# Transformer mixer layers on one core: order of one gather, one weight load and one weight split

## What is computed

```python
def _token_mix(h, w_in, w_out, gm_ln_g, gm_w_s, gm_b_s, da_lambda, da_sub_g, cmp_pe, cmp_w1, cmp_w2, lam_init):
    z = h @ w_in
    ...
    y_a = _gmlp_sgu(gu, gv, gm_ln_g, gm_w_s, gm_b_s)
    ...
    y_b = _diff_attention(dq, dk, dv, lam, da_sub_g, lam_init)
    y_c = _nsa(nq, nkc, nvc, nks, nvs, nkw, nvw, ng, cmp_pe, cmp_w1, cmp_w2)
    return jnp.concatenate([y_a, y_b, y_c], axis=-1) @ w_out

def _compress(x, pe, w1, w2):          # inside _nsa, for keys and for values
    ...
    blocks = x[:, :, idx] + pe
    flat = blocks.reshape(blocks.shape[0], blocks.shape[1], nc, CMP_LEN * HEAD_DIM_2)
    return jax.nn.silu(flat @ w1) @ w2
```

## Time and profile before

| | us |
|---|---|
| median of 3 runs | 2785.9 (2785.36 to 2786.52) |
| the profiled execution | 2786.57 |
| its span in the trace | 2785.2 |
| TensorE busy in it | 2715.7 |
| VectorE busy | 1667.7 |
| ScalarE busy | 1024.0 |

### The profile page before, as it was taken

How to read it: one execution, slowest core, us unless ns; L and a number is a source line. 1 busy time by engine, 2 the same in 40 slices (tenths; PEclk the granted TensorE clock), 3 DMA queues, 4 the chain that set the end, 5 groups by cost and what they waited for, 6 DMA issues and landing times.

```text
span 2785.2 us, 35300 instructions
## 1 busy us (share of the span) xinstructions
PE 2715.7 (98%) x14529; PEld 2222.0 (80%) x14529; DVE 1667.7 (60%) x3377; ACT 1024.0 (37%) x1745; POOL 15.8 (1%) x47
## 2 busy tenths in 40 slices
PE   8999999999999999899999999999999889999999
PEld 5788888898888897666888889888888666888888
DVE  6776565357767356777776746753355677633334
ACT  4642232444222244454422224322243455432223
POOL 1000000000000000000000000000000000000000
PEclk9999999999999999999999999999999999999999
DMA  7246333224555232201455524532232210123231
GB/s 248 91 167 183 106 98 96 72 91 167 200 190 170 93 107 84 94 18 46 166 182 186 192 83 147 193 130 97 93 115 84 88 46 31 61 92 106 91 102 65
DMA packets 340360, 325.24 MB, mean 117 GB/s; under 512 B 9442, under 2 KB 332774, under 8 KB 340200
## 3 DMA queue, kind: packets, MB, share of 16 engines
q1 hardware_dynamic: 340116, 322.97, 35.5%
q10 hardware_dynamic: 84, 0.02, 0.0%
HBM read 320.87 MB, written 2.10 MB: 116 GB/s over the span
## 4 chain that ended last, share of the span: by engine, by line
PE 89%; DVE 7%; ACT 2%; SPq 1%; issue 0%; DMA 0%; DVEq 0%
PE bank L529 25%; PE bank L531 24%; PE bank L530 24%; PE bank L571 3%; PE bank L557 2%; PE bank L559 2%; PE bank L558 2%; PE bank L2313 1%; PE bank L2342 1%; DVE w_lo L497 1%; PE bank L1367 1%; PE bank L1357 1%; ACT E L2116 1%; DVE tmp L707 1%; DVE h_lo L696 1%; PE bank L2019 0%
## 5 line engine op out<-in xcount | busy, mean ns | idle before, releaser
L529 PE MATMUL bank<-h_lo,w_hi 128*128 128x512 f32 (+1 forms) x2448 | 928.8, 379 | 7.7 <-DVE h_lo L696 7.3
L531 PE MATMUL bank<-h_hi,w_lo 128*128 128x512 f32 (+1 forms) x2448 | 902.3, 369 | 0.0
L530 PE MATMUL bank<-h_hi,w_hi 128*128 128x512 f32 (+1 forms) x2448 | 901.2, 368 | 0.0
L497 DVE TENSOR_TENSOR w_lo<-raw,w_hi 128x1024 fp32r<-128x1024 f32 (+1 forms) x422 | 491.1, 1200 | 300.8 <-ACT w_hi L491 300.6
L491 ACT ACTIVATE w_hi<-raw 128x1024 fp32r<-128x1024 f32 (+1 forms) x422 | 421.7, 1035 | 341.9 <-PE bank L531 326.5
L529 PEld LDWEIGHTS bank<-h_lo,w_hi 128*128 128x128 f32 x2448 | 462.7, 189 | 94.0 <-issue 9.8
L530 PEld LDWEIGHTS bank<-h_hi,w_hi 128*128 128x128 f32 x2448 | 462.7, 189 | 78.7 <-issue 6.9
L531 PEld LDWEIGHTS bank<-h_hi,w_lo 128*128 128x128 f32 x2448 | 462.1, 189 | 77.3
L529 PE MATMUL bank<-a_lo,w_hi 128*128 128x512 f32 (+1 forms) x1056 | 391.3, 371 | 0.0
L531 PE MATMUL bank<-a_hi,w_lo 128*128 128x512 f32 (+1 forms) x1056 | 384.9, 364 | 0.0
L530 PE MATMUL bank<-a_hi,w_hi 128*128 128x512 f32 (+1 forms) x1056 | 384.7, 364 | 0.0
(11 more groups left out here) (311 smaller groups left out, 2609.6 us busy)
## 6 DMA issues: line engine op xcount, KB each, us to landing
swf<-in_w_ada SPq DMA_DIRECT2D x60, 1024.0 KB, 7.3
raw<-in_ffn_w_gate SPq DMA_DIRECT2D x44, 1024.0 KB, 5.2
raw<-in_ffn_w_up SPq DMA_DIRECT2D x44, 1024.0 KB, 5.2
raw<-in_w_in SPq DMA_DIRECT2D x40, 1024.0 KB, 5.0
raw<-in_ffn_w_down SPq DMA_DIRECT2D x32, 1024.0 KB, 4.9
raw<-in_w_in SPq DMA_DIRECT2D x34, 512.0 KB, 5.0
raw<-in_ffn_w_down SPq DMA_DIRECT2D x16, 768.0 KB, 4.1
mw<-in_w_mod SPq DMA_DIRECT2D x8, 1024.0 KB, 11.1
```

Source lines behind the costliest of these rows:

```text
L497: nc.vector.tensor_tensor(o, r, half(w_his[place_of[i]], i, h)[0].bitcast(F32), ALU.subtract).then_inc(*w_lo.up((i, h)))
L529: nc.tensor.matmul(o, w1, al, start=start, stop=False)
L530: nc.tensor.matmul(o, w1, ah, start=False, stop=False)
L531: return nc.tensor.matmul(o, w2, ah, start=False, stop=stop)
```

## The change

Three edits, the same in both mixer layers. In `sp_raw` the load order swaps `w1 1 1` and `vv`; the buffers stay as they were. In `act_mixer` and `dve_mixer` the call that splits the last projection unit moves behind the last four attention steps. In `dve_mixer` the fourth gathered piece is emitted behind the third, before the silu, the split of `ng` and one attention step.

```diff
+    load_order = list(range(len(names)))
+    for l in range(2):
+        i = index["vv", l]
+        load_order[i - 1:i + 1] = [i, i - 1]
+
     def sp_raw(limit):
         while upto["sp"] <= min(limit, len(names) - 1):
-            i = upto["sp"]
+            i = load_order[upto["sp"]]
             parts, nk, n, kind = units[names[i]]
...
             for _ in range(7):
                 next(nsa)
-        act_w(("o2", l, 0))
         for _ in nsa:
             pass
+        act_w(("o2", l, 0))
         act_w(("o2", l, 1))
...
         gx1 = dve_gx(l, 1)
-        for _ in range(3):
+        for i in range(3):
             steps(1)
             next(gx1)
+        for _ in gx1:
+            pass
         dve_hidden_silu(l, 0)
         dve_w(("kk", l), 2, 0)
         steps(1)
-        for _ in gx1:
-            pass
         dve_rope(l, 8)
...
             dve_xup(st, ("o1", l, c), c, 2, gain)
-        dve_w(("o2", l, 0))
         for _ in nsa:
             pass
+        dve_w(("o2", l, 0))
         dve_w(("o2", l, 1))
```

## The result

| | before | after |
|---|---|---|
| median of 6 runs, us | 2785.77 (2785.36 to 2786.91) | 2774.73 (2774.22 to 2776.58) |
| ratio after / before | | 0.9961, 95% interval 0.9951 to 0.9971 |
| the profiled execution, us | 2786.57 | 2776.58 |
| its span in the trace, us | 2785.2 | 2775.2 |

The change saves 11.0 us. In the new kernel every line number stands 6 higher than before: the compression matmuls are L2182, the transposes L577, the rotation L1993 and L2004, VectorE's attention copy L2425, the dense product L535, the natural product L563.

What follows compares the result with a forecast made beforehand. TensorE, busy 2715.7 of 2785.2 us, bounds the kernel, so only its stalls and half clock offer time. Gains 1.8 + 4.0 + 5.0 + 0 = 10.8 us give 2775.8, less 0.7 for the median: 2775.1, range 2770.5 to 2780.

Steps and rivals of the forecast that it cites:

- The stall that goes and the wait that comes: Compression matmuls: the 5.97 us wait for gathered pieces goes; a 4.6 us wait for the rotation bank comes at rope 9.
- VectorE sets the next stage: After the gathered pieces, VectorE, with ScalarE in turns, sets the next stage, though TensorE gains 3.7 us at rope 9.
- Rival (b): Gather stall: the whole stall is freed if the rotation bank is free at 1130.3; 2761 us, chance 0.05.
- Part 1: Fourth gathered piece directly behind the third: gains 1.5 us in layer 0, 0.34 in layer 1, 1.8 us in all.
- The lower bound: Gather stage: gain 0 if the gate projection stays late because the half clock lasts longer than before.
- Part 2: Attention tail, last projection unit split when attention is done: gains 4.0 us in layer 0, 5.0 in layer 1.
- The halving: Tail, transposes to first dense product: 4.73 us at mostly half clock in layer 0 becomes 2.4 at full clock.
- the two hand-overs to VectorE's copies: Tail: two waits for VectorE's copies become visible in the faster run, priced at 0.3 us each.
- upper bound of 9.4 for the pair: Tails of both layers together: gain of at most 9.4 us, with no hand-over visible.
- Rival (a): Tail: the clock falls anyway because the work is thin; gain 6.4 us, 2779.5 us, chance 0.12.
- (c): Tail's next copies late for another reason and nothing from the gathered pieces: gain 2 to 4 us, 2783, chance 0.08.
- (d): Feed-forward up weights, loaded 5.4 us later, come late to the first gate and up products: 2790 us, chance 0.03.

Runs made afterwards that it cites:

- the kernel with the other bank: Changed kernel with rope 9 taking its bank from the dense products' set instead of the one rotation bank: 2775.11 us, ratio to before 0.9961.
- the silu in the waits: Changed kernel with the first set's silu moved into VectorE's waits for ScalarE in the attention steps ahead: 2773.21 us.
- part 1 alone: Kernel before with only the fourth gathered piece moved directly behind the third: 2784.83 us, ratio 0.9993.
- parts 1 and 2: Kernel before with the fourth gathered piece and the last projection unit's split both moved, load order unchanged: 2775.95 us, ratio 0.9962.
- part 2 alone: Kernel before with only the last projection unit's split moved behind the attention, on ScalarE and VectorE: 2778.05 us, ratio 0.9969.

## Why the prediction was right, point by point

The forecast was 2775.1, measured is 2774.7.

**The stall that goes and the wait that comes.** As forecast: no wait at the compression matmuls, and 4.35 us at the third rotation product in both layers (4.6 forecast, product at 1134.63 against 1134.9). TensorE was ready for it at about 1130.2, by the kernel with the other bank; 1130.3 was forecast. The second bank showed that this wait costs nothing of its own, so the step "VectorE sets the next stage" holds, and the silu in the waits confirms it from the other side: VectorE's work taken away came back as time. Rival (b) falls with it: its condition, the bank free early, was built, and gave nothing.

**Part 1, layer 0: 1.5 forecast.** 1.40 us with part 1 alone and 1.43 with parts 1 and 2, but 0.16 in the trace of the change. The step that was wrong is the reading behind it. I took most of the difference of the layers before (25.96 against 24.82; the 0.74 behind the reduction and the longer wait ahead of it) for a property of layer 0. It was a property of that execution: with the old order the stage took 24.53 in layer 0 of one trace and 25.76 in layer 1 of the same trace. The lower bound named the right cause, half clock that lasts, but I let it decide for the order after and not for the one before. The mean over the eight old stages is 25.20, over the five undisturbed new ones 24.55, so 0.65 for each layer or 1.3 us in all, by the traces. With layer 0 of the change counted in, which the old stages with a late clock would ask for, it is 24.76, so 0.44 for each layer or 0.9 in all. The medians gave 1.8 with an interval from about 4 us of gain to a small loss, so that they met the forecast's 1.8 is no proof of it.

**Part 2.** Forecast 4.0 and 5.0. Layer 0, by the rows: the transposes came 3.33 us behind the twelve value products and come 1.00 behind them, so 2.33 gained (2.28 forecast); from there to the dense product it was 4.73 and is 3.20, so 1.53 gained (1.68 forecast). Together 3.86. Layer 1, TensorE of the kernel before, and then after:

```profile
2375.85 0.88 PE L2342 MATMUL bank<-tmp,vsw 128*64 128x128 f32 x12
...
2403.21 0.60 PE L660 MATMUL bank<-nacc,res 128*128 128x256 f32 x2
```

```profile
2370.80 0.88 PE L2348 MATMUL bank<-tmp,vsw 128*64 128x128 f32 x12
2371.80 0.66 PE L577 MATMUL bank<-res,E 128*128 128x128 f32 x4
...
2375.00 0.50 PE L535 MATMUL bank<-a_lo,w_hi 128*128 128x512 f32 x1
...
2393.21 0.60 PE L666 MATMUL bank<-nacc,res 128*128 128x256 f32 x2
```

With the earlier trace rows: value products to transposes 3.34 before, 1.00 after, 2.34 gained; transposes to the dense product 5.47 before, 3.20 after, 2.27 gained (2.42 forecast); the dense products up to the sums 18.55 before (2384.66 to 2403.21), 18.21 after, 0.34 gained, which is the 0.3 forecast for the slow first ones. Together 4.95. The run from the transposes to the dense product is 3.20 where the sum had 3.05, and that they are so near is luck: two terms of it were wrong and cancelled. The halving was one. In layer 1 the same operations, with no wait among them in either trace, took 5.47 us with the clock at 0.50 and 3.20 at 1.00, so 1.7 times as long and not twice; in layer 0 the last 16 products ran at full clock already before (1317.21 to 1318.43, 1.22 us, as after), so only 3.51 of the 4.73 us were there to shorten. The other was the two hand-overs to VectorE's copies, 0.3 us each: no row of the tail after shows such a wait. The sum itself was written a little high too (2.4 and 0.6 make 3.0, not 3.05), and its upper bound of 9.4 for the pair doesn't follow from it: with no hand-over in either layer its own terms give about 10.2.

**Rival (a), the clock** in the tail, didn't come: 1.00 in the window of the tail. The rule of the Trainium skill, "TensorE: Matmul & The Clock Gate", section "Part 4: PE-mode transpose", that transposes don't count as busy for the clock as matmuls do, isn't contradicted by that and isn't tested: from 1309.34 to 1313.54 only 8 of 48 operations are transposes. The prediction spoke of transposes and small value products without counting them. No run here has transposes alone.

**Rivals (c) and (d).** No wait stands at the tail's copies. SyncE's next load shows when the last unit's split is done; SyncE, after:

```profile
1317.61 0.38 SPq L469 DMA_DIRECT2D raw<-in_ffn_w_up  x1
```

The unit's first product comes at 1324.58 (48 products behind 1313.54), so 7.0 us cover the split, 6.8 forecast. The load starts 4.4 us later than before by the trace's time, and 5.4 us later counted from the twelve value products (8.27 us behind them, 2.84 before), as forecast, and ScalarE splits what it brings from 1336.90 on, without a wait.

**The sum.** In the traces: 0.16 and 0.28 in the gather stages, 3.86 and 4.95 in the tails, 9.3 us; the rest of the 10.0 by which the spans differ lies where nothing was edited, most of it between the value weights and the tail of layer 0. Against it the medians differ by 11.0: the profiled execution lay 1.85 over its median after, 0.80 before. The forecast of 10.8 had 9.0 for the tails (8.8 in the traces, 8.6 by part 2 alone) and 1.8 for part 1 (1.6 in the trace of part 1 alone, 1.8 in its medians).

## What to carry to other kernels

When a wait that goes is replaced by another wait for the same engine one step on, as here, look whether that engine's order is the bound: take work off it, and only then look at banks and buffers again, which may count in the new balance though they gave nothing in the old. A block of weight splitting ahead of the attention copy that TensorE waits for cost its full length (2.3 us here, on VectorE; ScalarE's split, ahead of the other half of the copy, 0.6) and 1.5 to 2.6 us more behind it, where the clock had fallen; put it where TensorE has dense work for several microseconds. Before a difference between two layers or two traces is explained, look whether the granted clock differs, since the same order of work gave stages of 24.5 and 26.0 us.

## What the runs showed of the hardware

**VectorE is held up beside GpSimd.** While GpSimd added 64 x 512 blocks in SBUF, VectorE's two-input 128 x 512 multiplication went from 0.68 to 1.76 us, 1.08 more, less than one GpSimd addition (1.26 at least); the form that reads a bank didn't change (0.69). The Trainium skill, "SBUF — State Buffer", section "SBUF: two separate sides", says that VectorE's operations with two SBUF inputs and GpSimd's take one pair of ports as a lock for the whole instruction. The trace agrees with it: the delay stays under one instruction of the other engine, and the operation with one SBUF input is spared. Whether GpSimd's additions were held up as well can't be told, since no run has them alone. The move still paid, 3.4 us in the medians.

**The clock after one stall comes back at different times.** After the same stall of 5.97 to 5.99 us the granted clock was 0.50 until 10.2 to 11.4 us after the rotation product in five stages and until 16.0 to 16.4 in three, and the stage was 24.5 to 25.1 or 25.8 to 26.0 us long. The return goes with the fall: 3.4 to 4.6 us after the rotation product in the five, 5.8 to 6.2 in the three. Why the clock falls sooner or later within the same stall these runs don't show.
